# Attention scores of four heads at a time, in row tiles of the matmul array

## What is computed

```python
s = jnp.einsum('bqhd,bkhd->bhqk', qn, k_nope) + jnp.einsum('bqhr,bkr->bhqk', qp, k_pe)
s = jnp.where(k_pos[None, :] <= q_pos[:, None], s.astype(jnp.float32) * scale, -jnp.inf)
p = jax.nn.softmax(s, axis=-1).astype(v.dtype)
return jnp.einsum('bhqk,bkhd->bqhd', p, v)
```

## Time and profile before

| | us |
|---|---|
| runs, median of 3 | 2475.6 |
| lowest and highest run | 2467.85, 2475.68 |
| span of the profiled execution | 2472.7 |
| PE busy | 2222.6 |
| DVE, ACT, POOL busy | 1029.6, 866.3, 645.2 |

### The profile page before, as it was taken

One profiled execution on the slowest core, in us unless ns is written; L12 is line 12 of the kernel. 1 busy time (PEld: TensorE's weight loads), 2 busy tenths in 40 slices (PEclk: granted clock), 3 DMA queues, 4 the chain that ended last, 5 costly groups with the idle time before them and its releaser, 6 DMA issues. The chain is left out here.

```text
span 2472.7 us, 34704 instructions
## 1 busy us (share of the span) xinstructions
PE 2222.6 (90%) x10838; PEld 1261.5 (51%) x10839; DVE 1029.6 (42%) x2278; ACT 866.3 (35%) x2107; POOL 645.2 (26%) x1119
## 2 busy tenths in 40 slices
PE   6999999999947899999999995999948999999990
PEld 2545455554535566666666663455534444444440
DVE  2334343332435566666577654234352222222223
ACT  2264362552735454555555552111101010010012
POOL 1000001000024524633533500333211222222224
PEclk9999999999969999999999997999968999999995
DMA  9212121111173435434244216633303879999777
GB/s 332 87 63 73 52 75 61 51 63 35 62 196 99 116 111 151 127 107 134 77 138 137 70 52 251 221 136 111 128 34 111 254 221 272 303 325 296 215 225 297
DMA packets 224038, 362.77 MB, mean 147 GB/s; under 512 B 45675, under 2 KB 145670, under 8 KB 220438
## 3 DMA queue, kind: packets, MB, share of 16 engines
q1 hardware_dynamic: 210070, 310.62, 37.7%
q0 software_dynamic: 13824, 50.34, 8.4%
HBM read 260.97 MB, written 99.93 MB: 146 GB/s over the span
## 5 line engine op out<-in xcount | busy, mean ns | idle before, releaser
L692 PE MATMUL pV<-mod_rows_then_work,w_in_sb 128*128 128x512 f32 x768 | 340.1, 596 | 4.5 <-DMA w_in_sb<-in_w_in_dram 4.5
L2114 PE MATMUL hidden_ps<-w,keys_values_then_all 128*128 x752 | 331.6, 594 | 1.6 <-SPq L1986 1.6
L1465 PE MATMUL scores<-keys_values_then_all,queries 96*128 96x512 f32 (+3 forms) x640 | 299.8, 551 | 7.4 <-DMA keys_values_then_all<-kp_d 7.4
L1214 ACT ACTIVATE probs<-scores,neg_max 128x512 f32<-128x512 f32 (+3 forms) x320 | 199.7, 624 | 300.8 <-DVE neg_max L1323 204.0
L2114 PEld LDWEIGHTS hidden_ps<-w,keys_values_then_all 128*128 128x128 f32 x752 | 143.2, 191 | 182.2 <-issue 182.2
L692 PEld LDWEIGHTS pV<-mod_rows_then_work,w_in_sb 128*128 128x128 f32 x768 | 144.4, 191 | 177.4 <-issue 176.6
L1763 PE MATMUL out_ps<-keys_values_then_all 128*128 128x512 f32 x512 | 225.4, 598 | 2.8 <-ACT keys_values_then_all L1628 2.8
L1482 PE MATMUL outT_ps<-probs_T,keys_values_then_all 128*64 128x128 f32 x2176 | 158.6, 285 | 55.2 <-issue 36.0
L1470 PE MATMUL bank<-ident,probs 128*128 128x128 f32 x1088 | 184.3, 286 | 7.1 <-ACT probs L1214 6.7
L1323 DVE TENSOR_REDUCE neg_max<-scores 128x1 f32<-128x512 f32 x192 | 132.0, 687 | 137.0 <-PE scores L1465 136.0
L1482 PEld LDWEIGHTS outT_ps<-probs_T,keys_values_then_all 128*64 128x64 f32 x2176 | 120.9, 139 | 121.2 <-issue 98.1
(11 more groups left out here) (353 smaller groups left out, 3234.8 us busy)
## 6 DMA issues: line engine op xcount, KB each, us to landing
w<-in_w_dram SPq DMA_DIRECT2D x64, 1024.0 KB, 10.9
w_sb<-in_w_dram SPq DMA_DIRECT2D x32, 1024.0 KB, 14.1
w_mod_rows<-in_w_mod_dram SPq DMA_DIRECT2D x16, 1024.0 KB, 4.8
kqv<-qkv_d SPq DMA_DIRECT2D x16, 768.0 KB, 5.7
mod_rows_then_work<-in_w_mod_dram SPq DMA_DIRECT2D x4, 2048.0 KB, 14.9
x_in<-in_x_dram SPq DMA_DIRECT2D x16, 512.0 KB, 4.7
qkv_d<-l_out SPq DMA_DIRECT2D x32, 256.0 KB, 2.3
keys_values_then_all<-y_d SPq DMA_DIRECT2D x16, 512.0 KB, 4.9
```

Of the source, the lines that this page charges most:

```text
L692: last = pe.matmul(pV[n % 2][:], win[:, k, QKV0 + c * P:QKV0 + (c + 1) * P], hT[:, s % 2, k, :], start=(k == 0), stop=(k == ND - 1))
L1214: act.activation(prob[:, e, 0:w].rearrange("p t k -> p (t k)"), pS[e][:, 0:w * P], ACT.Exp, scale=-1.0, bias=nmin[:, i % 2, h, b:b + 1], a ...
L1465: pe.matmul(pS[e][:, 0:w * P], qT[:, i % 2, slot(h)], kT[:, 4 * b:4 * b + w, slot(h), :], start=True, stop=True).then_inc(s_ready, 1)
L2114: last = pe.matmul(pH[par][:], xT[par][:, k], m.w13[:, ds(slot, 1), k].rearrange("p s n -> p (s n)"), start=(k == 0), stop=(k == ND - 1))
```

## The change

Steps work on four heads. A quad j is half of the heads, a query tile and a key block, so there are 80 quads where there were 160 pairs; 56 have four key tiles, and eight each have one, two and three.

- S(j) issues eight products without a stop: first the four heads' rotary parts, each 32 rows in a row tile of its own (rows 0, 32, 64, 96) and each into a bank of its own (`scores0` to `scores3`), then the four plain parts, 64 rows each, in the two 64-row tiles, added on top. The signal for DVE comes after the second and the fourth head. S(j) waits until all four exponentials of the quad before are done.
- DVE's reduction and ACT's exponential of heads 0 and 1 stand behind S, those of heads 2 and 3 behind the two V steps of quad j-1.
- The four T steps stand together, then S, then V of heads 0, 1 and V of heads 2, 3. ACT copies heads 0 and 2, DVE heads 1 and 3. The copy of the output products is one for four heads.
- Score banks: four. Turning banks: three. The two O steps of a quad stand together.
- Keys and queries lie in SBUF by head pairs (plain, 128 rows) and four times or four heads (rotary, 32 rows each). `load_k` has five transfers as before, the rotary ones first and half as large. The query weights load in 6 transfers instead of 12, without reordering of heads.
- The inversion's work area moves, two DeltaNet buffers become one (`Wb = Yb`), and SP waits for the last inverses before it loads the output weights. The costs in the list are 0.13 for a transposition (0.11), 0.66 for a quad's scores (0.88 for four heads) and 0.26 for V (0.22), each per key tile.

```diff
-    pairs = [(i, hp, b) for i in range(NT) for hp in range(AH // 2) for b in range(TILE[i] // 4 + 1)]
+    quads = [(i, qd, b) for i in range(NT) for qd in range(AH // 4) for b in range(TILE[i] // 4 + 1)]
     atoms = []
-    for j, (i, hp, b) in enumerate(pairs):
+    for j, (i, qd, b) in enumerate(quads):
         n = min(4, TILE[i] + 1 - 4 * b)
-        ahead = min(4, TILE[pairs[j + 1][0]] + 1 - 4 * pairs[j + 1][2]) if j + 1 < len(pairs) else 0
-        for e in range(2):
-            atoms.append((0.11 * n, [("T", j, e)]))
-            if ahead:
-                atoms.append((0.22 * ahead, [("S", j + 1, e), ("X", j + 1, e)]))
-            if i and (i, hp, b) == (i, 0, 0):
+        ahead = min(4, TILE[quads[j + 1][0]] + 1 - 4 * quads[j + 1][2]) if j + 1 < len(quads) else 0
+        first, last = (qd, b) == (0, 0), (qd, b) == (AH // 4 - 1, TILE[i] // 4)
+        for e in range(4):
+            atoms.append((0.13 * n, [("T", j, e)]))
+            if i and first and e < 2:
                 atoms.append((0.0, [(("BX", "B2")[e], i - 1, 0)]))
-        o = j - pairs.index((i, 0, 0))
-        if i and o < AH // 2:
-            atoms.append((0.11 * (TILE[i - 1] // 4 + 1), [("O", i - 1, o)]))
-        atoms.append((0.22 * n, [("V", j, 0)]))
-        if i and o == AH // 2 - 1:
+        if ahead:
+            atoms.append((0.66 * ahead, [("S", j + 1), ("X", j + 1, 0), ("X", j + 1, 1)]))
+        o = j - quads.index((i, 0, 0))
+        if i and o < AH // 4:
+            for hp in (2 * o, 2 * o + 1):
+                atoms.append((0.13 * (TILE[i - 1] // 4 + 1), [("O", i - 1, hp)]))
+        for p in range(2):
+            atoms.append((0.26 * n, [("V", j, p)] + [("X", j + 1, 2 + p)] * (ahead > 0)))
...
+KP_W, KN_W = NT * P, NT * AH // 2 * P
+KV_W = 16384
...
-    NBANK = 5
+    NBANK = 3
...
-        kT = m.kv[0:QK, 0:KV_W].rearrange("p (t h k) -> p t h k", t=NT, h=AH)
+        kP = m.kv[:, 0:KP_W].rearrange("p (t k) -> p t k", t=NT)
+        kN = m.kv[:, KP_W:KP_W + KN_W].rearrange("p (t b k) -> p t b k", t=NT, b=AH // 2)
         v = m.kv[:, KV_W:].rearrange("p (t n) -> p t n", t=NT)
-        qT = sb("queries", [QK, 2, AH, P])
+        qN, qP = sb("queries", [P, 2, AH // 2, P]), sb("rope_queries", [P, 2, AH // 4, P])
...
-        prob, probT = sb("probs", [P, 2, 4, P]), sb("probs_T", [P, 2, 2, 4, P])
+        prob, probT = sb("probs", [P, 4, 4, P]), sb("probs_T", [P, 4, 4, P])
...
-        pS = [ps(f"scores{e}", [P, 512]) for e in range(2)]
-        pO = ps("outT_ps", [P, 4, P])
+        pS = [ps(f"scores{e}", [P, 512]) for e in range(4)]
+        pO = ps("outT_ps", [P, 2, P])
...
-                    i, hp, b = pairs[n]
-                    w, h = width(n), 2 * hp + e
-                    wait(min_ready, 2 * n + e + 1)
-                    wait(t_ready, 2 * n + e - 1)
+                    i, qd, b = quads[n]
+                    w, h = width(n), 4 * qd + e
+                    wait(min_ready, 4 * n + e + 1)
+                    wait(t_ready, 4 * n + e - 3)
                     if i >= 2:
                         wait(wgt_ready, i - 1)
                     act.activation(prob[:, e, 0:w].rearrange("p t k -> p (t k)"), pS[e][:, 0:w * P], ACT.Exp, scale=-1.0,
                                    bias=nmin[:, i % 2, h, b:b + 1], accum_out=sums[:, i % 2, h, b:b + 1]).then_inc(exp_done, 1)
...
-                elif kind == "S":
+                elif kind == "X":
                     e = step[2]
-                    i, hp, b = pairs[n]
-                    w, h = width(n) * P, 2 * hp + e
-                    wait(s_ready, 2 * n + e + 1)
+                    i, qd, b = quads[n]
+                    w, h = width(n) * P, 4 * qd + e
+                    wait(s_ready, 2 * n + e // 2 + 1)
...
-                    e = step[2]
-                    i, hp, b = pairs[n]
-                    w, h = width(n), 2 * hp + e
-                    if (hp, b, e) == (0, 0, 0):
+                    i, qd, b = quads[n]
+                    w = width(n)
+                    if (qd, b) == (0, 0):
                         wait(q_loaded[i % 2], 32 * (i // 2 + 1))
                         if i in first_use:
-                            s = first_use.index(i)
-                            wait(k_loaded[s], 16 * (1 + KV[s + 1] - KV[s]))
-                    wait(exp_done, 2 * n + e - 1)
-                    pe.matmul(pS[e][:, 0:w * P], qT[:, i % 2, slot(h)], kT[:, 4 * b:4 * b + w, slot(h), :], start=True, stop=True).then_inc(s_ready, 1)
+                            wait(k_loaded[first_use.index(i)], 16 * 5)
+                    wait(exp_done, 4 * n)
+                    for e in range(4):
+                        pe.matmul(pS[e][:, 0:w * P], qP[row32[e], i % 2, qd], kP[row32[e], 4 * b:4 * b + w], start=True, stop=False)
+                    for e in range(4):
+                        hp = 2 * qd + e // 2
+                        last = pe.matmul(pS[e][:, 0:w * P], qN[row64[e % 2], i % 2, hp], kN[row64[e % 2], 4 * b:4 * b + w, hp],
+                                         start=False, stop=True)
+                        if e % 2:
+                            last.then_inc(s_ready, 1)
```

More of the change, by code:

```diff
@@ L344, in _ @@
                 elif kind == "WS":
[L345 removed]
+                    act.wait_ge(up_loaded, 16 * 6)
                     act.wait_ge(cols_made, 1)
@@ L779, in mix_order @@
         order += kinds
-    return pairs, order
+    return quads, order
 MIX_LEAD = 1.0
@@ L1472, in _ @@
                 elif kind == "V":
-                    i, hp, b = pairs[n]
+                    i, qd, b = quads[n]
+                    u, hp = 2 * n + step[2], 2 * qd + step[2]
                     for e in range(2):
-                        wait(t_copied[e], n + 1)
-                    wait(oT_copied, n - 3)
+                        wait(t_copied[e], u + 1)
+                    wait(oT_copied, n)
                     if (hp, b) == (0, 0) and i in first_use:
```

91 lines of the change are left out of this document (42 added, 49 removed).

## The result

The changed kernel takes 2558.7 us (median of 4 runs, 2555.3 to 2562.9), the kernel before 2475.3 us beside it: a ratio of 1.0346, interval 1.0326 to 1.0365. It is slower by 83 us where 14 was forecast. The sign was right and the time lies 1 us inside the upper end of the range; the size was not seen. The profiled execution spans 2556.0 us against 2472.7.

A forecast was written before the change was run, and what follows sets the result against it. PE was taken as the bound in the mixed attention and DeltaNet stage. The terms -58.5 + 9.5 + 22 + 24 + 10 + 7 gave +14 us, hence 2490 us, with a range of 2430 to 2560 us.

The forecast's parts named there:

- Streaming: Score products: row tiles run together, saving 0.215 us on each of 272 quad-tiles, 58.5 us in all.
- rival without overlap: Score products: tiles do not run together, scores take 234 us more, about 2650 us in all; chance 0.07.
- Mode changes: PE's tiling switches: neighbours with different tilings go from 450 to 523, at 0.13 us each, +9.5 us.
- The waits: New PE waits in the mixed stage: full quads +22, held banks +24, first quads +10, narrow quads +7 us.
- Faster: Mixed stage: PE's cover is longer than laid out, waits of 10 us in place of 63, 2437 us; chance 0.33.
- held banks: A chunk's K and KS hold turning banks, so transpositions wait: +2 us for each of 12, +24 us.
- two weightings at a query tile's first quad: Two weightings ahead of head 2's reduction, where one stood before: about +0.8 us for 13 tiles, +10 us.
- one quad's 0.5 us: Full quads: third transposition waits for the first one's copy, 0.5 us for 44 of 56 quads, +22 us.
- No change: Mixed stage: waits are 49 us and cancel the rest, 2476 us; chance 0.10.
- block length: Sign of being right: a full score block takes 2.6 us plus 0.3.
- PE's busy time falls by 30 us or more: Sign of being right, on PE: its busy time drops by at least 30 us.
- most at the chunks' K: Sign of being right: new PE waits before the transpositions (L1473) come mostly at the DeltaNet chunks' K products.

The follow-up runs named there:

- e9: The changed kernel with each of the four rotary products run over all 128 rows, one after another; 2728.3 us, ratio 1.1043 to the kernel before.
- e8: The changed kernel without the rotary products of the scores; 2490.6 us, ratio 1.0062 to the kernel before.
- e11: e6 with K and KA moved behind VT, KD, KS and QS, and the list's costs set near the traced lengths; 2443.7 us.
- e12: The kernel before with only K and KA moved behind VT, KD, KS and QS; 2453.1 us, ratio 0.9924 to the kernel before.
- e3: The changed kernel with reductions and exponentials of all four heads directly behind the scores; 2510.2 us, ratio 1.0154 to the kernel before.
- e4: The changed kernel with the score block between second and third transposition, exponentials of heads 2 and 3 behind those transpositions; 2488.8 us.
- e2: The changed kernel with K next to KA and KS next to QS, so banks are held more briefly; 2522.8 us.
- e6: The changed kernel with the edits of e4 and e2, plus one output transposition ahead of each output product; 2470.1 us.
- e7: The changed kernel with all four heads' rotary products in row tile 0, one after another; 2898.4 us, ratio 1.1740 to the kernel before.

## Why the prediction was right and wrong

- **Streaming, -58.5 us: right.** The score block takes 2.99 us (above), and in e9 and e8 the stage moves by most of the PE time that they add and take away (149 of 157, 63 of 74). The rival without overlap falls with it.
- **Mode changes, +9.5 us: too small. This is one of two steps that failed.** The count was right (the traces have 450 before and 523 after; e11 has 574), the price was not. A row-tiled pass has 0.21 us above its streaming, not 0.13. Two of them in 80 blocks are 0.16 x 80 = 13 us more, and the entry into the block is booked on the step ahead of it. The cleanest pair is e12 and e11, at one clock (0.96). Taken from start to start in the timeline, without the idle time, the score blocks fall from 258.1 to 215.4 us there. That is 42.7 of the 58.5 us; 16 go to the passes' own overhead. The transpositions rise from 133.3 to 146.6 us. Start to start at full clock, one followed by another takes 0.11 us, one followed directly by a tiled step 0.20, and one behind which PE waits 0.27 (to its modelled end). The second kind goes from 38 to 86 and the third from 1 to 41, 11 us together. In all the busy time falls by 17.7 us in this pair, not 49: some 31 us of the forecast's saving do not show. Full-clock work says the same of the changed kernel: 714.4 us before, 696.4 after, 18 less. In all seven kernels that reorder its steps it is 692 to 698. So what stands beside the streaming grew by some 40 us, where 9.5 were forecast. The Trainium skill (TensorEngine Tiling, Key Properties) says that a change of tiling mode drains TensorE. The 0.21 us of a pass agree with it.
- **The waits, +63 us: right in place and cause, in sum by luck.** PE's idle time in the stage rose by 61.4 us. But before transpositions it rose by 105 us, released by ACT's and DVE's copies, and by some 23 before other steps, while 55 us before output products and 12 at the stage's end went away, of which the sum knew nothing (the rival *Faster* named new waits that take the place of old ones). That the order of the copies costs is shown by e3 and e4, the held banks by e2, the two weightings at a query tile's first quad by e6. How the 61 us split over the terms is not shown: each edit takes busy time along with the idle time, and their gains overlap. It was not one quad's 0.5 us that counted: of 97 waits before transpositions, 17 of over 2 us hold 54 of the 111 us.
- **The clock: no term in the sum. This is the other step that failed, and the larger one.** The prediction read 0.98 in the earlier trace rows and carried it over. The lower level cost PE 23.8 us of the stage before (738.2 - 714.4) and 60.8 after (757.2 - 696.4), **37 us** more. Part of it is seen in the timeline: the transpositions, which stand behind the waits, go from 135.6 us before to 173.0 after for the same work from start to start, idle time left out. Of this rise of 37 us 11 are clock; 26 remain at full clock, 18 of them because 112 transpositions now stand ahead of a wait, where 2 did. In e4 the clock of 860 to 1490 us is back at 0.98 and they take 155.5; in e11 0.99 and 146.6.
- **The sum again,** with what was found: 14 - 2 (idle time) + 31 (work beside the streaming) + 37 (clock) + 3 (outside the stage) = 83, as measured. The range held the time only because the upper bounds of the waits were added up in it; they stood in for causes that had no term or too small a one.
- **The rivals.** *Faster* turned on cover of over 3.8 us between the scores and the third transposition. The changed order does not have it; e4, e6 and e11 put the score block itself between the second and the third transposition. *No change* needed 49 us of waits and no loss of clock.
- **The signs to look for.** Right: tiles together, block length, waits before L1473. Wrong: "PE's busy time falls by 30 us or more" (it rose by 24 in the whole program), and "most at the chunks' K", which e2's 36 us against the 49 and 70 of e3 and e4 do not bear out, though e2's figure is net of the 20 us that it brings. And the wait of 2.44 us that the prediction puts behind DVE is put down to "issue" in the earlier trace rows, not to DVE.

Still open: why the clock falls with the waits (the runs show that it falls behind them, and that it returns when they go), how the 61 us split over the terms, and what the kernel before would gain from fitted costs.

## What to carry to other kernels

Row tiles save what the streaming says, if PE is the bound, less about 0.2 us for each pass and what the entries and new waits add to the steps around: here 58.5 us of streaming became 17 to 22 us of PE's work. And making the step larger changes the list that three in-order engines follow. Before making it, lay the chain of the last part of the larger step against the work behind it, and see that no copy which frees a bank stands behind that chain. And price a wait on PE at more than its length: look at the granted clock just behind the waits that the trace already has.

## What had not been expected of the hardware

- Behind waits of 2.73 and 2.04 us the granted clock was 0.50, and eight transpositions took 1.76 us instead of 0.88. Over the stage the mean clock went from 0.94 to 0.91 and, in the best order, to 0.96. Beside 61 us more of idle time the lower level cost 37 us more.
- Behind 32-row float32 products one after another the clock fell to 0.50 with PE busy for 6.61 of the last 6.70 us (e7); behind full-height products of the same length it did not at the block shown (e9). The stage differs by 145 us for it; the clock of 860 to 1490 us is 0.82 in e7 and 0.95 in e9. With four row tiles side by side it is 1.00 over the score block shown, as the 1.92 us of the plain pass also say.
- A row-tiled pass of float32 products with four tiles took 1.07 us for 0.86 of streaming, one with two tiles 1.92 for 1.71: the same 0.21 us each.
